# Reordering the first and the last pair of experts in a one-core mixture-of-experts layer

## What is computed

```python
def routed_ffn(h, p):
    logits = tok @ router_w + router_b
    top_val, top_idx = lax.top_k(logits, 4)
    gate = softmax(top_val)
    ...
    # for each expert e and the tokens xb that chose it, with their gates g:
    gu = xb @ w_gu[e] + b_gu[e]                       # 1024 -> 2048
    x_glu = minimum(gu[:, :1024], 7.0)
    x_lin = clip(gu[:, 1024:], -7.0, 7.0)
    act = x_glu * sigmoid(1.702 * x_glu) * (x_lin + 1.0)
    out = (act @ w_down[e] + b_down[e]) * g           # 1024 -> 1024
    ...
    # y = sum over experts; then x + gate2 * rms_norm(y)
```

## Time and profile before

| | us |
|---|---|
| median of 3 runs | 1206.25 (1206.07 to 1207.28) |
| the profiled execution | 1206.84 |
| its span, first to last instruction | 1205.0 |
| TensorE busy | 1123.2 (93%) |
| VectorE, ScalarE, POOL busy | 393.8, 199.2, 68.1 |
| read from HBM | 454.13 MB |

### The profile page before, as it was taken

How to read it: one execution, slowest core, us unless ns; L and a number is a source line. 1 busy time by engine, 2 the same in 40 slices (tenths; PEclk the granted TensorE clock), 3 DMA queues, 4 the chain that set the end, 5 groups by cost and what they waited for, 6 DMA issues and landing times.

```text
span 1205.0 us, 16442 instructions
## 1 busy us (share of the span) xinstructions
PE 1123.2 (93%) x6676; PEld 510.6 (42%) x6676; DVE 393.8 (33%) x935; ACT 199.2 (17%) x458; POOL 68.1 (6%) x113
## 2 busy tenths in 40 slices
PE   4999999999999999898999999999999898989997
PEld 2886776744434333333333333344333333333432
DVE  0598887654321212121212121213212121212123
ACT  2311344423111110101010101011111111110102
POOL 1003444400000000000000000000000000000000
PEclk9999999999999999999999999999999999999999
DMA  9900746888999999999999999999999999999995
GB/s 369 386 29 10 311 174 247 311 308 327 423 413 432 432 432 427 430 429 430 431 431 430 431 430 431 419 424 432 431 431 430 431 432 430 430 432 424 427 425 243
DMA packets 39948, 456.11 MB, mean 379 GB/s; under 512 B 5168, under 2 KB 5696, under 8 KB 16352
## 3 DMA queue, kind: packets, MB, share of 16 engines
q1 hardware_dynamic: 39112, 454.58, 90.0%
q0 software_dynamic: 480, 0.80, 0.2%
q10 hardware_dynamic: 312, 0.11, 0.0%
HBM read 454.13 MB, written 1.34 MB: 378 GB/s over the span
## 4 chain that ended last, share of the span: by engine, by line
PE 50%; DMA 44%; DVE 4%; issue 1%; ACT 1%; SPq 0%; DVEq 0%; ACTq 0%
DMA ring<-in_w_gu 39%; PE bank L637 24%; PE bank L675 5%; PE bank L757 5%; DMA front<-in_w_down 3%; DMA ring<-in_ada_w 2%; PE bank L1028 2%; PE bank L592 2%; PE bank L582 1%; PE bank L752 1%; PE bank L872 1%; PE bank L767 1%; PE bank L814 1%; PE bank L887 1%; PE bank L617 1%
## 5 line engine op out<-in xcount | busy, mean ns | idle before, releaser
L637 PE MATMUL bank<-ring,front 128*64 128x512 f32 x2032 | 461.3, 609 | 36.0 <-DMA ring<-in_w_gu 36.0
L637 PEld LDWEIGHTS bank<-ring,front 128*64 128x64 f32 x2032 | 143.9, 140 | 351.2 <-issue 283.8
L1521 DVE TENSOR_SCALAR front<-bank 128x512 f32<-128x512 f32 x32 | 22.1, 692 | 481.6 <-PE bank L637 481.6
L675 PE MATMUL bank<-front 128*64 128x512 f32 x512 | 113.6, 595 | 9.5 <-ACT front L1159 9.1
L675 PE MATMUL bank<-ring,front 128*64 128x512 f32 x512 | 113.4, 595 | 5.1 <-ACT front L1159 5.1
L1151 ACT ACTIVATE front<-front 128x512 f32<-128x512 f32 x32 | 20.2, 631 | 488.1 <-DVE front L1521 488.1
L1545 DVE COPY front<-bank 64x512 f32<-64x512 f32 x32 | 21.9, 683 | 175.1 <-PE bank L675 175.1
L675 PEld LDWEIGHTS bank<-front 128*64 128x64 f32 x512 | 36.3, 137 | 76.5 <-issue 73.3
L675 PEld LDWEIGHTS bank<-ring,front 128*64 128x64 f32 x512 | 36.3, 137 | 71.9 <-issue 70.4
L592 PE MATMUL bank<-front 128*128 128x512 f32 x136 | 62.9, 605 | 1.5 <-DVE front L1545 1.5
L582 PE MATMUL bank<-front 128*128 128x128 f32 x480 | 56.0, 275 | 0.0
(11 more groups left out here) (272 smaller groups left out, 901.6 us busy)
## 6 DMA issues: line engine op xcount, KB each, us to landing
ring<-in_w_gu SPq DMA_DIRECT2D x46, 4096.0 KB
front<-in_w_down SPq DMA_DIRECT2D x30, 2048.0 KB, 19.5
ring<-in_w_down SPq DMA_DIRECT2D x28, 2048.0 KB, 20.2
ring<-in_w_gu SPq DMA_DIRECT2D x25, 2048.0 KB
ring<-in_ada_w SPq DMA_DIRECT2D x24, 1024.0 KB, 11.7
ring<-in_w_gu SPq DMA_DIRECT2D x20, 1024.0 KB
ring<-in_w_in SPq DMA_DIRECT2D x5, 2048.0 KB, 19.9
ring<-in_w_down SPq DMA_DIRECT2D x6, 1024.0 KB, 10.1
```

What stands on the lines that cost most here:

```text
L637: last = pe.matmul(ps[r][64 * hf:64 * hf + 64, :], xT[:, k, S * q:S * q + S], rows, start=False, stop=(k == order[-1]))
L675: last = pe.matmul(ps[2][64 * c:64 * c + 64, :], actT[:, m, 64 * hf:64 * hf + 64], wdn[q][hf][:, m, c * 512:(c + 1) * 512], start=(k == 0) ...
L1521: v.tensor_scalar(glu, ps[0], 7.0, None, ALU.min).then_inc(s["glu_ready"], 1)
```

## The change

- In the first pair TensorE does gate/up of both experts, the second in banks 6 and 7, and then both downs (`pe_first`). Combine number 1 is gone. Act of expert 0 is turned within expert 1's gate/up.
- Chunks 6 and 7 of expert 0 are loaded to `r_rk` and `r_a` (`lent`), which are dead once h2 is written; chunks 6 and 7 of expert 1 go into the ring. `w_out`'s places are refilled one chunk at a time. In `load_first` expert 2's other chunks come ahead of its down.
- `b_down` is loaded twice by POOL, to `bdn`, without the clearing. The gates of all experts are transposed by a matmul and kept in `gates_T`. `put_sums` stands ahead of the last pair and adds four matmuls, gates by down biases, to the sums.
- In the last pair (`pe_last`) the order is: sums, gate/up of expert 30, combine, act of expert 30 turned, gate/up of expert 31, gates and act of expert 31 turned (`actT2`), down of expert 30, down of expert 31 into bank 0. SP loads gate/up of expert 31 ahead of the down of expert 30, and the last down half in three pieces (2, 1, 1 chunks).
- TensorE loads the largest count (`more`), which decides the branch, ahead of the last pair.
- VectorE and ScalarE have a first, a middle and a last form of their part of a pair; the four additions of combine number 1 are gone, and `yacc` is cleared within the first pair.

```diff
+        lent = {KC - 2: r_rk, KC - 1: r_a}
+        SECOND_ORDER = (0, 1, 4, 5, 6, 7, 2, 3)
...
+        bdn, gates_T = r_ra[2 * E:4 * E, 0:D], r_E[2 * E:4 * E, 512:640]
...
+        actT2 = view(r_kk[:, 512:1024], "p (m s) -> p m s", m=4)
...
-            sp.wait_ge(s["wout_half"], 1)
-            load_gu_part(sp, 0, 4, 1, 32)
-            sp.wait_ge(s["mix_mm"], 2 * G)
-            load_gu_part(sp, 0, 6, 1, 32)
+            for k in range(4, KC):
+                if k < KC - 1:
+                    sp.wait_ge(s["wout_part"], k - 3)
+                else:
+                    sp.wait_ge(s["mix_mm"], 2 * G)
+                load_gu_part(sp, 0 if k < 6 else 1, k, 1, 16, 1)
             sp.wait_ge(s["x1_ss"], 4)
             for hf in range(2):
                 load_spare(2, 1, hf)
+            sp.wait_ge(s["h2"], 2 * G)
+            for k, home in lent.items():
+                sp.dma_start(home, gu_src(0, k, k + 1)[:, 0, :]).then_inc(in_gu[5], 16)
...
-                for k in range(4, KC):
+                for k in range(4, 6):
                     sp.wait_ge(s["gu_used"], k + 1)
-                    load_gu_part(sp, 1, k, 1, 16, 1)
-                fine_dn(0, 2, 0)
-                for n, k in enumerate((0, 1, 4, 5, 6, 7)):
+                    load_gu_part(sp, 1, k, 1, 32, 1)
+                for n, k in enumerate(SECOND_ORDER):
+                    if k in (2, 3):
+                        continue
                     sp.wait_ge(s["gu_used"], KC + n + 1)
                     load_gu_part(sp, 2, k, k // 4, 32 if k < 4 else 16, 1)
+                fine_dn(0, 2, 0)
                 fine_dn(1, 3, 1)
                 fine_gu(2, 3)
...
-                    next_dn(base + e - 2, e, e % 2)
+                    if e == E - 3:
+                        next_dn(base + e - 2, e, 1)
+                next_dn(base + E - 4, E - 2, 0)
+                sp.wait_ge(s["dn_used"], (base + E - 3) * KC + 4)
+                load_dn(sp, E - 1, 1, 0)
+                sp.wait_ge(s["dn_used"], (base + E - 3) * KC + KC)
+                for m0, m1, arrived in ((0, 2, in_dn[1][1]), (2, 3, in_last_dn[0]), (3, 4, in_last_dn[1])):
+                    sp.dma_start(wdn[1][1][:, m0:m1, :], dn_src(E - 1, 1)[:, m0:m1, :]).then_inc(arrived, 16)
...
+        def put_sums(pe, with_bias):
+            for n in range(4):
+                g, c = divmod(n, 2)
+                if with_bias:
+                    pe.matmul(ps[4 + n], gates_T[E * g:E * g + E, :], bdn[E * g:E * g + E, c * 512:(c + 1) * 512],
+                              start=True, stop=False)
+                pe.matmul(ps[4 + n], ident, yacc[:, g, c * 512:(c + 1) * 512], start=not with_bias, stop=True)
...
+        def lent_rows(k, r, hf):
+            return lent[k][:, r * F + hf * 512:r * F + hf * 512 + 512] if k in lent else ring_rows(k, r, hf)
+        def spare_rows(k, r, hf):
+            return spare[k - 2][r][hf] if k in (2, 3) else ring_rows(k, r, hf)
...
+        def pe_first(pe):
+            pe.wait_ge(s["bsel_ready"], 1)
+            bias_rows(pe, 0, ps[0:2])
+            pe.wait_ge(s["xt_ready"], 2)
+            for k in range(KC):
+                if k % 4 == 0:
+                    pe.wait_ge(in_gu[k // 4], 80)
+                if k == KC - 2:
+                    pe.wait_ge(in_gu[5], 112)
+                gate_up(pe, 0, k, lent_rows, KC - 1, ps[0:2])
+            bias_rows(pe, 1, ps[6:8])
+            pe.wait_ge(s["gate"], 2)
+            for g in range(G):
+                last = pe.matmul(ps[5][(2 + g) * E:(3 + g) * E, 0:T], gate[:, g, 0:E], ident, start=True, stop=True)
+            last.then_inc(s["gate_tr"], 1)
+            for n, k in enumerate(SECOND_ORDER):
+                if k % 4 == 0:
+                    pe.wait_ge(in_gu[k // 4], 144)
+                if k in (2, 3):
+                    pe.wait_ge(in_gu[3 + k], 80)
+                if n == KC - 1:
+                    pe.wait_ge(in_gu[7], 80)
+                gate_up(pe, 1, k, spare_rows, SECOND_ORDER[-1], ps[6:8])
+                if n == 3:
+                    pe.wait_ge(s["act_ready"], 1)
+                    turn_act(pe)
+            for k in range(KC):
+                if k in (0, 2):
+                    pe.wait_ge(s["actT_ready"], k // 2 + 1)
+                if k % 4 == 0:
+                    pe.wait_ge(in_dn[0][k // 4], 64)
+                down(pe, ps[2], actT, 0, k)
+            pe.wait_ge(s["glu_ready"], 2)
+            pe.wait_ge(s["selg_ready"], 1)
+            turn_gates(pe, ps[6])
+            pe.wait_ge(s["act_ready"], 2)
+            turn_act(pe)
+            pe.wait_ge(s["gt_ready"], 1)
+            gather(pe, 2)
+            for k in range(KC):
+                if k in (0, 2):
+                    pe.wait_ge(s["actT_ready"], 2 + k // 2 + 1)
+                if k % 4 == 0:
+                    pe.wait_ge(in_dn[1][k // 4], 48)
+                down(pe, ps[7], actT, 1, k)
...
+        def pe_last(pe, base, turn=None):
...
+            put_sums(pe, with_bias=turn is None)
+            pe.wait_ge(s["bsel_ready"], n + 1)
+            for q in range(2):
+                if q == 1:
+                    pe.wait_ge(s["act_ready"], n * 2 + 1)
+                    turn_act(pe)
+                    pe.wait_ge(s["actT_ready"], n * 4 + 2)
+                bias_rows(pe, q, ps[0:2])
+                for k in range(KC):
+                    if k % 4 == 0:
+                        pe.wait_ge(in_gu[k // 4], arrived[q])
+                    if k in (2, 6):
+                        pe.wait_ge(in_gu[2 if k == 2 else 3], late_turn * 96 + (32 * (2 + q) + 16))
+                    if k == 7 and q == 1:
+                        pe.wait_ge(in_gu[4], late_turn * 32 + 48)
+                    gate_up(pe, q, k, ring_rows, KC - 1, ps[0:2])
+                if q == 0:
+                    combine(pe, n + 1, on_sums=True)
+            pe.wait_ge(s["selg_ready"], n + 1)
+            pe.wait_ge(s["glu_ready"], n * 2 + 2)
+            turn_gates(pe, ps[0])
+            pe.wait_ge(s["act_ready"], n * 2 + 2)
+            turn_act(pe)
+            for q, out, turned in ((0, ps[2], actT), (1, ps[0], actT2)):
+                if q == 1:
+                    pe.wait_ge(s["gt_ready"], n + 2)
+                for k in range(KC):
+                    if k in (0, 2):
+                        pe.wait_ge(s["actT_ready"], n * 4 + (2 * q + k // 2 + 1))
+                    if k % 4 == 0:
+                        pe.wait_ge(in_dn[q][k // 4], arrived_dn[q])
+                    if q == 1 and k >= 6:
+                        pe.wait_ge(in_last_dn[k - 6], late_turn * 16 + 32)
+                    down(pe, out, turned, q, k)
...
-                if (k, g) == (Q - 1, 1):
-                    last.then_inc(s["wout_half"], 1)
+                if g == 1 and k in (1, 3, 5):
+                    last.then_inc(s["wout_part"], 1)
...
-            pe.wait_ge(s["gate"], 2)
-            for g in range(G):
-                last = pe.transpose(ps[6][0:E, g * P:(g + 1) * P], gate[:, g, 0:E], ident)
-            last.then_inc(s["gate_tr"], 1)
-            pe.wait_ge(s["in_bdn"], 16)
-            pe_pair(pe, 0, 0, first=True)
+            pe_first(pe)
             with pe.Fori(1, E // 2 - 2) as i:
                 pe_pair(pe, 0, i)
-            pe_pair(pe, 0, E // 2 - 2, late=(1,))
-            pe_pair(pe, 0, E // 2 - 1, last_pair=True, late=(0, 1))
+            pe_pair(pe, 0, E // 2 - 2, late=(1, 0))
             pe.wait_ge(s["flag"], 1)
             more = pe.value_load(most_i[P - 1:P, 0:1], min_val=0, max_val=N)
-            with pe.If(more > S):
+            pe_last(pe, 0)
+            with pe.If(more < S + 1):
+                pe.wait_ge(s["gt_ready"], E // 2 + 1)
+                combine(pe, E // 2 + 1, on_sums=True)
+            with pe.Else():
...
-            po.wait_ge(s["mix_mm"], 2 * G)
-            po.memset(outp, 0.0).then_inc(s["outp_ready"], 4)
-            po.memset(GT, 0.0).then_inc(s["cleared"], 1)
-            po.wait_ge(s["outp_ready"], 4)
-            po.dma_start(outp[0:E, :], b_down).then_inc(s["in_bdn"], 16)
+            for g in range(G):
+                po.dma_start(bdn[E * g:E * g + E, :], b_down).then_inc(s["in_bdn"], 16)
...
+        def dve_first(v):
+            gate_act(v, 0, 0)
+            gated_choice(v, 0)
+            choose(v, 1)
+            v.memset(yacc, 0.0)
+            gate_act(v, 0, 1, (ps[6], ps[7]))
+            v.wait_ge(s["dn_used"], 1)
+            choose_bias(v, 1)
+            take_down_v(v, 0, 0, ps[2])
+            take_down_v(v, 0, 1, ps[7])
...
+        def dve_last(v, base):
+            n = base + (E // 2 - 1)
+            gate_act(v, n, 0)
+            v.wait_ge(s["gt_tr"], n)
+            gated_choice(v, E // 2 - 1)
+            gate_act(v, n, 1)
+            take_down_v(v, n, 0, ps[2])
+            take_down_v(v, n, 1, ps[0])
...
+        def act_last(a, base):
+            n = base + (E // 2 - 1)
+            gate_sigmoid(a, n, 0)
+            take_act(a, n, 0, actT)
+            gate_sigmoid(a, n, 1)
```

(36 more changed lines are left out.)

218 lines of the change are left out of this document (108 added, 110 removed).

## The result

The changed kernel took 1213.07 us (1212.74 to 1215.37, 4 runs) beside 1206.16 (1205.67 to 1207.28, 4 runs) for the kernel before: ratio 1.0057, interval 1.0041 to 1.0073. It is slower, and 4 us above the range that was forecast. Measured again, ten runs against 27, it took 1209.19 beside 1206.99: 1.0017 (1.0001 to 1.0032), still 0.4 us above the range. So the sign is the same twice, and the size lies between 2 and 7 us. Single executions spread: the ten of the changed kernel over 6 us, the 27 of the kernel before over 8.

The account below looks back on a forecast made before the run. The prediction held the middle to be bound by transfers. Terms of -4.2 and +3.5 us took the span from 1205.0 to 1204.3; -0.7 on the median 1206.25 gave 1205.5 us, range 1201.8 to 1208.8.

Parts of the forecast that it names:

- -4.2: Start of the experts: rows loaded early put the queue ahead, a lead kept to the last wait; -4.2 us, bounds 1.0 to 5.7.
- +3.5: Last pair: the new order, with biases added to the sums, makes the end later by 3.5 us, bounds +1.0 and +4.3.
- S: Mark: first bias rows of expert 0, at 285.50 us before; forecast some 0.3 us earlier.
- S to L: From expert 0's first bias rows to the last pair's first matmul: forecast -3.1 us.
- L to C: From the last pair's first matmul to the last combine: forecast +2.6 us.
- 11.0 MB at 419 GB/s is 26.3 us, to 304.9: First pair: with the queue fed from 278.6 us, lent rows, down half, spare and six rows finish at 304.9 us.
- the first pair gives the lead back: Slower rival: late rows 4 and 5 of expert 1, or a gap at 330 us, cost 3 us; 1208.7 us, chance 0.10.
- Sums, 7.2 us: Start of the last pair: eight matmuls, four sums and four new biases, at line 592's price, 3.6 us per four.
- The new hole, 2.82 + 0.6: Last pair: expert 31's act transposes wait ahead of down 30; rival that the clock falls there: +1.7 us, chance 0.15.
- The clock behind the wait at 1090.73: Faster rival: TensorE's clock stays up in the half of expert 28 there, 1.7 us less; 1203.8 us, chance 0.15.
- The branch: Count load moved ahead of the last pair: up to 0.8 us saved before last combine, the same 0.8 charged ahead.
- The last bytes set the end: Faster rival: the last transfer's landing sets the end, with less down work behind it; 1199.4 us, chance 0.10.

Follow-up runs that it names:

- other row order: The changed kernel with expert 1's chunks used in the order 0, 1, 6, 7, 4, 5, 2, 3: 1207.94 us, ratio 1.0002.
- The grouped run: The changed kernel with the four down-bias matmuls first, one behind the other, then the four sums: 1207.06 us, ratio 1.0001.
- three mended kernels: Changed kernel with new row order, moved act transposes, grouped biases: 1201.49 us; then biases in pair 13's combine: 1201.28; then half of down 30 issued earlier: 1201.43.

## Why the prediction was wrong

The sum was -4.2 and +3.5. The three profiles of each kernel give -0.4 and +5.0, and +1.6 ahead of both. By the three marks the forecast had -0.3 for S, -3.1 for S to L (the lead, with 0.8 added for the load of the count) and +2.6 for L to C. So it missed by 1.9, 2.7 and 2.4 us: about a third of the whole lies at each place.

- **"11.0 MB at 419 GB/s is 26.3 us, to 304.9", and chunks 4 and 5 "landing at about 305 when they are wanted": this step failed.** They are the last of those bytes, and TensorE went on at 309.20. Measured from S, which the forecast had at 285.2, the forecast is 19.7 us and the run 22.2; the second and third profiles have 22.2 as well, and the runs with act transposes moved and with grouped biases 22.2 and 22.1, so it is no accident. Two stretches of the first profile, from where the forecast has the queue fed (6.6 us ahead of S), to the forecast's landing and to the real one:

```profile
280.40:306.70 26.30, 25.64 (x157) 11.14 (x156) 9.57 (x41) 4.92 (x10) 0.00 (x0) 1.00 1.01 408
280.40:309.20 28.80, 25.85 (x157) 11.14 (x156) 10.99 (x41) 4.92 (x10) 0.00 (x0) 1.00 1.00 401
```

Of the 2.5 us the rate, 408 GB/s instead of the 419 of a full queue, is 0.3 MB or 0.7 us. By 309.20, though, 401 x 28.8 = 11.5 MB had moved, 0.5 more than the 11.0 counted: 1.3 us of bytes that, by the times of issue, can only belong to the rows issued behind them, from 305.24 on. The forecast let the transfers land one behind the other. They overlap: of two issued at 282.45 and 282.82 us the second landed at 292.20 and the first at 292.84. The last 0.5 us the runs don't divide. The step had no slack, so nearly all of the 2.5 us became a wait, 2.3 us; the queue lives on chunks being used, so a late TensorE is a late queue. The run with the other row order shows it by its reversal: its lead is 6.4 us, and 4.0 to 5.7 in the three mended kernels behind it, in the mean 5.4 of four profiles against 0.9 of the five with the wait. My 4.2 lies at the lower edge of what those four show, and was wrong as what the forecast's order of rows lets through.
- **The rival "the first pair gives the lead back" is what happened**, at the place that it named (rows 4 and 5), with the point that it gave: the lead is under 1.1 and the kernel is slower. I gave it 0.10 with the remark that the margins were under 1 us, and that remark should have set its chance: the forecast needed all of them to hold, and a miss of one costs its own size at once. Its price, 1208.7, was still low, since it had the last pair and the start at the forecast's sizes.
- **Sums, 7.2 us: 8.43.** Line 592's price (0.89 us each) is that of one shape in a row. That row showed nothing of alternation, where each matmul takes 1.05; the bound 1.1 us for four was wrong the other way, since side by side they take 1.9. The Trainium skill, page "TensorE: Matmul & The Clock Gate", section "Why this matters for your kernels", holds that the gain of small row groups lies in tiles running together. The grouped run agrees (0.48 us each against 1.05).
- **The new hole, 2.82 + 0.6: 2.15 idle behind 0.41 of gates, and transposes 1.04.** The size was right. But I priced the hole and its clock as separate cases, the second with 0.15. The clock fell behind such a hole in the last pair in five of six profiles that have one (not with grouped biases), and in none of the four without. In my own rows [5, 11] such a wait had its fall behind it. It costs 1.6 us here (16.99 against 15.42 from the transposes to C), since nothing swallows it, and belonged in the sum.
- **The clock behind the wait at 1090.73** fell as before in the first profile (at 1091.9 us), and the rival that it would stay up is refuted there; it had no effect that the marks show.
- **The branch.** The idle time ahead of the last combine fell from 1.51 to 0.88 us, 0.6 of the 0.8 forecast. It is 0.87 or 0.88 in every profile with the load moved, and 1.51, 1.32 and 2.78 in the three of the kernel before. The load ahead of the pair cost nothing visible: sums follow down of expert 29 without a gap.
- **"The last bytes set the end"** was refuted for this change: no wait for a transfer in the last pair, and the queue had air (401 GB/s from 1100 to 1180 us, before 427), since the chunks of expert 31 wait for those of expert 30 to be used. It is what stops the kernel with the biases taken early.
- **Ahead of the experts** I counted -0.3 us and found +1.2 to +2.0 (S in the table), of which no part was forecast. Its cause stays open.

The last pair's 62.55 us by these: my 59.2, and 0.7 to combine, make 59.9; sums add 1.2, the clock 1.6, and the hole with the gates was 0.3 shorter (1181.54 to 1184.10): 62.4. What stays open is the size: with +5.0 in every profile's last pair, the second set of timed runs shows only +2.2 us in the median. Its profiled execution took 1213.79, the longest of its ten, so the profiles may stand for the upper part of them. The record has the mean granted clock of each timed run: it is 0.983 to 0.985 in the six of the changed kernel that took 1212.7 us or more, and 0.985 to 0.988 in the eight others. So the slower executions had more time at the lower clock; whether it was in the hole isn't shown.

## What to carry to other kernels

Where each transfer waits for the use of the last one, a reordering must be laid out chunk by chunk with the rate of a queue that is just filling, with room for transfers that overlap, and the consumer should first take what landed long ago: with the row order as built the new first pair gave a lead of 0.9 us in the mean, with four numbers of it swapped and a semaphore for the late chunks 5.4. Price a hole in TensorE together with the slow stretch behind it, and fill it with the work that follows, split in two. Keep small matmuls of different row groups together, apart from full ones, or put them ahead of a wait that exists anyway, and stop when the transfers become the bound.

## What the runs showed of the hardware

- A float32 matmul of 32 rows by 128 columns over 512 took 1.05 us from start to start between full ones, as did the full ones between them (0.89 in a row of their own), and 0.48 when four in alternating row groups stood together.
- Waits of 2.0 to 2.6 us were enough to bring TensorE to 1.2 GHz for 3.4 us, often but not always: behind 2.15 or 2.16 us in the same place of the last pair it fell in five profiles and stayed in one. Behind the waits for chunks 4 and 5 (2.2 to 2.3 us) it fell in one profile of five.
- Up to 10.2 us at 1.2 GHz fell into the first 36 us of some executions and none into others, among kernels whose code there is the same; with it went a start of the experts between 285.5 and 288.8 us.
- Transfers of one queue overlapped: one issued 0.37 us behind a larger one landed 0.64 us ahead of it (292.20 and 292.84 us), and by the landing of 11.0 MB of rows 11.5 MB had moved.
